# Delta net stage: inverse in two groups, scan without W and U, output norm token-major

## The reference, cut to what matters

```python
a_strict = jnp.einsum('bhnid,bhnjd->bhnij', kb, k) * decay * (idx[:, None] > idx[None, :])
rhs = jnp.concatenate([v * beta[..., None], kb * jnp.exp(gc)[..., None]], axis=-1)
sol = lax.linalg.triangular_solve(a_strict + jnp.eye(C, dtype=F32), rhs, left_side=True, lower=True, unit_diagonal=True)
u, w = sol[..., :dv], sol[..., dv:]
attn = jnp.einsum('bhnid,bhnjd->bhnij', q, k) * decay
def step(S, inp):
    v_new = u_i - jnp.einsum('bhcd,bhde->bhce', w_i, S)
    o = (jnp.einsum('bhcd,bhde->bhce', q_i * jnp.exp(g_i)[..., None], S)
         + jnp.einsum('bhij,bhje->bhie', a_i, v_new))
    S = (S * jnp.exp(g_last)[..., None, None]
         + jnp.einsum('bhcd,bhce->bhde', k_i * jnp.exp(g_last[..., None] - g_i)[..., None], v_new))
    return S, o
```

## Time and profile before

| | |
|---|---|
| median of 3 runs | 2707.88 us (2705.71 to 2708.81) |
| span of the profiled execution | 2700.6 us |
| TensorE busy | 2612.6 us, 97% of the span |
| VectorE, ScalarE, GpSimd busy | 1011.4, 660.8, 501.4 us |

### The profile page before, as it was taken

One profiled execution on the slowest core, in us unless ns is written; L12 is line 12 of the kernel. 1 busy time (PEld: TensorE's weight loads), 2 busy tenths in 40 slices (PEclk: granted clock), 3 DMA queues, 4 the chain that ended last, 5 costly groups with the idle time before them and its releaser, 6 DMA issues. The chain is left out here.

```text
span 2700.6 us, 43745 instructions
## 1 busy us (share of the span) xinstructions
PE 2612.6 (97%) x17527; PEld 1664.5 (62%) x17528; DVE 1011.4 (37%) x2331; ACT 660.8 (24%) x1383; POOL 501.4 (19%) x465
## 2 busy tenths in 40 slices
PE   6999999979999999999999999999997999999998
PEld 3565565555555555556677677767744458568485
DVE  2354455346676763013444344434432110010100
ACT  3354454121222210115222332323202111110110
POOL 0111111132332315222223122312200100000000
PEclk7999999989999999999999999999998999999999
DMA  8234224113333342201011101110209997695841
GB/s 250 69 78 128 68 68 126 48 52 119 109 109 115 105 118 64 65 22 34 3 32 33 32 2 33 33 32 2 72 17 348 344 343 226 186 296 176 253 130 28
DMA packets 321292, 295.01 MB, mean 109 GB/s; under 512 B 5920, under 2 KB 285600, under 8 KB 321024
## 3 DMA queue, kind: packets, MB, share of 16 engines
q1 hardware_dynamic: 315648, 273.17, 33.3%
q0 software_dynamic: 4352, 15.60, 2.4%
q10 hardware_dynamic: 1152, 4.19, 0.4%
HBM read 279.83 MB, written 11.53 MB: 108 GB/s over the span
## 5 line engine op out<-in xcount | busy, mean ns | idle before, releaser
L2363 PE MATMUL bank<-hidden,weight_ring 128*128 128x512 f32 (+1 forms) x768 | 308.7, 536 | 1.8 <-ACT work L2707 1.8
L1293 PE MATMUL bank<-hidden,weight_ring 128*128 128x384 f32 x704 | 237.7, 491 | 4.9 <-ACT hidden L415 4.9
L648 PE MATMUL bank<-weight_ring,hidden 128*128 128x384 f32 x672 | 237.2, 496 | 1.6 <-ACT work L795 1.4
L1439 DVE SCALAR_TENSOR_TENSOR weight_ring<-weight_ring,silu_c 128x256 f32<-128x256 f32 x308 | 213.7, 735 | 5.5
L1293 PEld LDWEIGHTS bank<-hidden,weight_ring 128*128 128x128 f32 x704 | 132.9, 191 | 93.5 <-issue 6.7
L2363 PEld LDWEIGHTS bank<-hidden,weight_ring 128*128 128x128 f32 x768 | 134.9, 190 | 82.4 <-issue 68.1
L1293 PE MATMUL bank<-weight_ring 128*128 128x384 f32 x528 | 181.6, 494 | 0.3 <-DVE work L1447 0.3
L648 PEld LDWEIGHTS bank<-weight_ring,hidden 128*128 128x128 f32 x672 | 121.7, 191 | 92.1 <-issue 15.7
L1810 PE MATMUL bank<-work,weight_ring 128*128 128x224 f32 x768 | 147.7, 354 | 0.0
L1810 PEld LDWEIGHTS bank<-work,weight_ring 128*128 128x128 f32 x768 | 144.1, 190 | 1.9 <-ACT work L1892 1.6
L1293 PEld LDWEIGHTS bank<-weight_ring 128*128 128x128 f32 x528 | 99.3, 192 | 70.1 <-issue 5.9
(11 more groups left out here) (386 smaller groups left out, 3994.8 us busy)
## 6 DMA issues: line engine op xcount, KB each, us to landing
weight_ring<-in_moe_w_in SPq DMA_DIRECT2D x64, 1024.0 KB, 9.5
weight_ring<-in_ada_w SPq DMA_DIRECT2D x38, 1024.0 KB, 5.3
weight_ring<-in_ffn_w_in SPq DMA_DIRECT2D x44, 512.0 KB, 4.9
hidden<-in_moe_w_out SPq DMA_DIRECT2D x8, 2816.0 KB, 10.0
residual<-in_moe_w_out SPq DMA_DIRECT2D x8, 2816.0 KB, 14.6
work<-in_moe_w_in SPq DMA_DIRECT2D x16, 1024.0 KB, 8.4
weight_ring<-in_na_w_qkv SPq DMA_DIRECT2D x24, 512.0 KB, 9.5
weight_ring<-in_gdn_w_qkv SPq DMA_DIRECT2D x24, 512.0 KB, 5.4
```

The costliest lines, as they stand in the source:

```text
L648: mm = nc.tensor.matmul(m.psum[6][:, 0:3 * P], m.H[:, k, t * P:(t + 1) * P], weights(u)[:, k, :], start=(k == 0), stop=(k == KD - 1))
L1293: mm = nc.tensor.matmul(bank[:, 0:HT], w[:, k, :], t[:, k, :], start=(first and k == 0), stop=(last and k == HK - 1), skip_group_check=True)
L1439: nc.vector.scalar_tensor_tensor(out=out, in0=ada_slab[:, k, :], scalar=by, in1=out, op0=ALU.mult, op1=ALU.add).then_inc(acc_ok, 1)
L2363: mm = nc.tensor.matmul(B[b][:, c0:c0 + t1 - t0], W[:, s, k, :], m.H[:, k, t0:t1], start=(k == 0), stop=(k == KD - 1))
```

## The change

1. **Inverse.** LEVELS = 6 becomes GROUPS = 2. The first mask gives U = I - A0 as before. A group then does Y = AM T, and three nested products (`xa`, `xb`, `xc`: X = U - Y U, X = U - Y X, U = U - Y X) and the same last product for T; after two groups one more Y and one `u`. GpSimd makes four masks per direction, not six, each in its own buffer.
2. **Scan without W and U.** `wt`, `cu`, `kb`, `vb` and the two turns `at0`, `at1` go. A step is now `ks` (keys times state), `x` on VectorE (V - e^g k S), `tx` on TensorE (inverse times x), `vn` on ScalarE (scaled copy), `kv`, `st`.
3. **k and q of a chunk as one stationary operand.** From step 4 on `ks` multiplies keys and queries (`KQ`, 128 columns) with the state at once; the query half is taken by `oa` on ScalarE (steps 4 to 7) or `od` on VectorE (steps 8 to 11), and `eg`, `QE` and their exponentials go.
4. **Output norm token-major.** Squares with sums on ScalarE, the scaling on GpSimd, four transposes (`turn_out`), and the gate's product on VectorE; `norm_sums` and `norm_rows` go.
5. The streams are rewritten in a new order; the output weights of the last turn are loaded in two batches.

```diff
-LEVELS = 6
+GROUPS = 2
...
+                def ks(s):
                     if not scan:
                         return
-
+                    for d in range(2):
+                        t, half, _, c, _ = place(s, d)
+                        pe.wait_ge(dve_scan_step, VS.before(h, f"st{s - 1}.{d}"))
+                        if s < 4:
+                            k0 = t * P + CH * half
+                            mm = nc.tensor.matmul(B[SCAN + d][c, 0:P], keys(h - 1)[:, k0:k0 + CH], state[:, d, :], start=True, stop=True)
+                        else:
+                            mm = nc.tensor.matmul(B[SCAN + d][:, 0:P], keys_and_queries(h - 1, t, half), state[:, d, :], start=True, stop=True)
+                        mm.then_inc(pe_scan_step, TS.step(f"ks{s}.{d}"))
...
+                def tx(s):
...
+                            pe.wait_ge(dve_scan_step, VS.before(h, f"x{s}.{d}"))
+                        x = xs[c, d, :] if s else V[(h - 1) % 2][c, t, :]
+                        nc.tensor.matmul(B[SCAN + d][c, 2 * P:3 * P], UF[c, n, :], x, start=True, stop=True)\
+                            .then_inc(pe_scan_step, TS.step(f"tx{s}.{d}"))
...
+                        _, _, n, c, _ = place(s, d)
+                        pe.wait_ge(act_scan_step, SS.before(h, f"vn{s}.{d}"))
+                        if s >= MEET:
+                            pe.wait_ge(dve_scan_step, VS.before(h, f"od{s}.{d}"))
+                        if s < STEPS - 1:
+                            nc.tensor.matmul(B[SCAN + d][:, P:2 * P], kd[c, n, :], vn_[c, d, :], start=True, stop=True)\
...
+                            t, _, _, c, other = place(s, d)
+                            nc.tensor.matmul(B[OUT][other, t * P:(t + 1) * P], AT[c, 4 * d + t, :], vn_[c, d, :], start=(s == 4), stop=True,
...
+                def turn_out():
...
+                    pe.wait_ge(pool_scan_step, GS.before(h, "on"))
                     for t in range(4):
...
+                        mm = nc.tensor.transpose(B[GATE][:, t * P:(t + 1) * P], otok[:, t, :], ident)
...
+                    mm = nc.tensor.transpose(B[(0, 2)[t // 4]][:, (t % 4) * P:(t % 4 + 1) * P], keys(h)[:, t * P:(t + 1) * P], ident)
                 mm.then_inc(pe_step, TE.step("kt"))
-                pe.wait_ge(dve_step, VE.after(h, "right_vc"))
+                ks(5)
...
                 mm.then_inc(pe_step, TE.step("kk"))
-                ws(5)
-                project(1, 0, 0, CTX, TOK, 4, 6)
-                kv(5)
-                project(1, 0, 0, CTX, TOK, 6, 8).then_inc(pe_step, TE.step("q"))
-                ws(6)
+                tx(5)
                 pe.wait_ge(act_step, SC.after(h, "Kc"))
                 project(2, 0, 2, CTX, TOK, 0, 2)
+                kv(5)
+                project(2, 0, 2, CTX, TOK, 2, 4)
+                ks(6)
+                project(2, 0, 2, CTX, TOK, 4, 6)
+                tx(6)
+                project(2, 0, 2, CTX, TOK, 6, 8).then_inc(pe_step, TE.step("v"))
                 kv(6)
...
+                gate_part(0, 2)
+                ks(7)
+                pe.wait_ge(act_step, SC.after(h, "silu_q1"))
+                pe.wait_ge(dve_step, VE.after(h, "a1"))
...
+                ks(8)
+                pe.wait_ge(dve_step, VE.after(h, "U0"))
+                turn(0, U, 0, "tt0")
...
+                def first(g, d):
...
+                    multiply(2 * d, AM[g + 1], T, d, f"y{g}.{d}")
+
+                def second(g, d):
+                    pe.wait_ge(act_step, SC.after(h, f"Y{g}.{d}"))
+                    multiply(2 * d + 1, Y, U, d, f"xa{g}.{d}")
+
+                def third(g, d):
+                    pe.wait_ge(dve_step, VE.after(h, f"Xa{g}.{d}"))
+                    multiply(2 * d, Y, X, d, f"xb{g}.{d}")
+
+                def fourth(g, d):
+                    pe.wait_ge(dve_step, VE.after(h, f"Xb{g}.{d}"))
+                    multiply(2 * d + 1, Y, X, d, f"xc{g}.{d}")
+                    multiply(2 * d, X, Y, d, f"t{g}.{d}")
...
+                third(0, 0)
+                ks(11)
+                third(0, 1)
+                tx(11)
+                fourth(0, 0)
+                kv(11)
+                fourth(0, 1)
...
-                            b = (1, 0)[d] + 2 * half
-                            mm = nc.tensor.matmul(blocks(b, TILES)[:, n, :], kb[c, TILES * d + n, :], U[c, TILES * d + n, :],
-                                                  start=True, stop=True)
-                    mm.then_inc(pe_step, TE.step(f"wt{d}"))
...
-                        for c in HALF_ROWS:
-                            mm = nc.tensor.matmul(B[b][c, at_:at_ + P], U[c, TILES * d + n, :], vb[c, TILES * d + n, :], start=True, stop=True)
-                    mm.then_inc(pe_step, TE.step(f"cu{d}"))
+                    third(1, d)
...
+                    pe.wait_ge(act_step, SC.after(h, f"Y{GROUPS}.{d}"))
+                    pe.wait_ge(dve_step, VE.after(h, f"Xc{GROUPS - 1}.{d}"))
+                    multiply(1 + d, Y, U, d, f"u.{d}")
+                turn_out()
...
+                def oa(s):
...
+                        act.wait_ge(pe_scan_step, TS.before(h, f"ks{s}.{d}"))
+                        nc.scalar.activation(oacc[other, t, :], B[SCAN + d][other, 0:P], ACT.Identity, scale=coef[other, EGS, h - 1, n:n + 1])\
+                            .then_inc(act_scan_step, SS.step(f"oa{s}.{d}"))
+
+                def vn(s):
...
+                    for d in range(2):
+                        _, _, n, c, _ = place(s, d)
+                        act.wait_ge(pe_scan_step, TS.before(h, f"tx{s}.{d}"))
+                        nc.scalar.activation(vn_[c, d, :], B[SCAN + d][c, 2 * P:3 * P], ACT.Identity, scale=hr[(h - 1) % 2][c, 0, n:n + 1])\
+                            .then_inc(act_scan_step, SS.step(f"vn{s}.{d}"))
...
+                oa(5)
                 act.wait_ge(pe_step, TE.after(h, "kt"))
                 act.wait_ge(pool_step, GP.before(h, "kd1"))
                 for t in range(4):
-                    op = nc.scalar.activation(k_sq[:, t, :], B[0][:, t * P:(t + 1) * P], ACT.Square, accum_out=ss_k[:, t:t + 1])
+                    op = nc.scalar.activation(k_sq[:, t, :], B[0][:, t * P:(t + 1) * P], ACT.Square, accum_out=nk[h % 2][:, t:t + 1])
                 op.then_inc(act_step, SC.step("sq_k"))
+                vn(5)
+                for t in range(2):
+                    op = nc.scalar.activation(k_sq[:, 4 + t, :], B[2][:, t * P:(t + 1) * P], ACT.Square, accum_out=nk[h % 2][:, 4 + t:5 + t])
+                op.then_inc(act_step, SC.step("sq_kc"))
+                act.wait_ge(act_step, SC.after(h, "sq_kc"))
+                nc.scalar.activation(nk[h % 2], nk[h % 2], ACT.Sqrt, bias=const(m, C_EPS, 1)).then_inc(act_step, SC.step("root_k"))
                 nc.scalar.copy(K[:, 0:4, :], B[0][:, :].rearrange("p (n t) -> p n t", n=4)).then_inc(act_step, SC.step("K"))
-                for t in range(2):
-                    op = nc.scalar.activation(k_sq[:, 4 + t, :], B[2][:, t * P:(t + 1) * P], ACT.Square, accum_out=ss_k[:, 4 + t:5 + t])
-                op.then_inc(act_step, SC.step("sq_kc"))
                 nc.scalar.copy(K[:, 4:6, :], B[2][:, 0:2 * P].rearrange("p (n t) -> p n t", n=2)).then_inc(act_step, SC.step("Kc"))
-                act.wait_ge(act_step, SC.after(h, "sq_kc"))
-                nc.scalar.activation(ss_k, ss_k, ACT.Sqrt, bias=const(m, C_EPS, 1)).then_inc(act_step, SC.step("root_k"))
...
-                    nc.vector.tensor_tensor(T[:, of(d), :], blocks(3, TILES), DM[:, of(d), :], ALU.mult).then_inc(dve_step, VE.step(f"ad{d}"))
-                vn(7)
-                for d in range(2):
-                    dve.wait_ge(pe_step, TE.after(h, f"at{d}"))
-                    nc.vector.tensor_tensor(A[:, of(d), :], blocks(d, TILES), spread(hr[:, 0, of(d)], TILES, CH), ALU.mult)\
-                        .then_inc(dve_step, VE.step(f"a{d}"))
...
+                nc.vector.tensor_scalar(qn[h % 2], B[3][:, CTX:CTX + 4], float(GD * GD * EPS), None, ALU.mult).then_inc(dve_step, VE.step("qn"))
+                x(8)
+                od(8)
                 for d in range(2):
                     dve.wait_ge(pool_step, GP.after(h, f"am0.{d}"))
-                    nc.vector.tensor_tensor(T[:, of(d), :], same(ident64, TILES), AM[:, of(d), :], ALU.subtract)\
...
+                    nc.vector.tensor_tensor(U[:, of(d), :], same(ident64, TILES), AM[0][:, of(d), :], ALU.subtract).then_inc(dve_step, VE.step(f"U{d}"))
...
+                x(11)
+                od(11)
+                take_b(0, 0)
+                take_b(0, 1)
                 sum_o()
-                level(2)
-                value_rows(0)
-                value_rows(1)
-                level(3)
-                value_rows(2)
+                take_c(0, 0)
+                take_c(0, 1)
...
+                for d in range(2):
+                    take_a(1, d)
+                for d in range(2):
+                    take_b(1, d)
```

(16 more changed lines are left out.)

829 lines of the change are left out of this document (414 added, 415 removed).

## The result

The changed kernel takes 2715.75 us (median of 7 runs, 2714.88 to 2720.19), the kernel before, beside it on the same chip, 2707.88 (2705.71 to 2710.42): ratio 1.0033, 95% interval 1.0023 to 1.0043. The forecast was 2686 and faster. The value lies inside the range, by 1.25 us, and the sign was wrong. In the profiled executions the spans are 2714.0 and 2700.6 us, a difference of 13.4. Of the four executions of the later run e9_all one, 3257.59 us at a granted clock of 0.745, was in a slower state of the chip and counts in no ratio.

What follows compares the result with a forecast made beforehand. TensorE's issue time bounds a middle turn: 91.5 us less 13.1 of work and the 0.17 wait, plus 9.7 of waits and 1.4 of clock, makes 89.3. With turn 0 (-4) and the last (-1): 2686 us, range 2640 to 2717.

Steps and rivals of the forecast that it cites:

- What bounds it, and that the cover decides: A middle turn is TensorE's issue time; removing its instructions pays only while waits between the engines keep their cover.
- Kc: TensorE's wait for ScalarE's copy of the transposed keys, ahead of the v projection: 3.3 us a turn.
- a1: TensorE's wait behind `ks` of step 7 for VectorE's second a tile: 1.7 us a turn.
- U0: TensorE's wait behind `ks` of step 8 for VectorE's first U tile: 1.7 us a turn.
- `x` of step 5: TensorE's wait for VectorE's x, which stands behind q's convolution: 0.4 us a turn.
- so I add 1.4 a turn: TensorE's clock halves behind the Kc wait, slowing the work that follows: 1.4 us a turn.
- the clock falls at every wait: Rival, chance 0.12: the clock also falls at a1, U0 and in the inverse; 93.5 us a turn, 2721, slower.
- dm1's wait: `tx` replaces `kv` and the table load loses the cover of `eg`: 0.4 us a middle turn.
- 0.06 per change: Price of a change of TensorE's tiling mode between projections and scan steps: 0.06 us, judged a small thing.
- Turn 0: The first turn loses work, its own waits and slow stretch but gains new waits and clock loss: net -4 us.
- work kept: Rival, chance 0.10: the waits overlap more than laid out; 2598 with none, 2640 with half of them.
- longer chain of the scan: Rival, chance 0.06: the scan's four hops for two set the pace; the gain is gone, 2708.

Runs made afterwards that it cites:

- e9_all: e6_both and e8_o_late together, plus two VectorE subtractions of the inverse moved ahead of od(11) and sum_o; 2611.78 us, ratio 0.9649 to the kernel before.
- e3_fill: Changed kernel with four unread 512-column matmuls in TensorE's queue ahead of the wait for the copy of the keys; 2701.1 us, ratio 0.9974 to the kernel before.
- e6_both: Changed kernel with keys transposed ahead of half of q's projection and a and U tiles earlier on VectorE; 2630.33 us, ratio 0.9725 to the kernel before.
- e10_kv_twice: e9_all with the pair of state products kv of steps 0 to 10 issued twice; 2627.55 us, ratio 0.9705 to the kernel before.
- e8_o_late: Changed kernel with the output products o of a step right ahead of the next step's tx; 2696.69 us, ratio 0.9967 to the kernel before.
- e1_kc_order: Changed kernel with ScalarE copying the transposed keys out before it takes the root of their norms; 2695.91 us, ratio 0.9952 to the kernel before.
- e2_kt_early: Changed kernel with keys transposed ahead of half of q's projection, ScalarE's squares and copies and VectorE's x(5) earlier; 2661.55 us, ratio 0.9828 to the kernel before.

## Why the prediction was wrong, step by step

- **What bounds it, and that the cover decides:** right. All time went and came in TensorE's turns.
- **The waits:** right in place and releaser, and nearly in size: Kc, a1, U0 and `x` of step 5 forecast 3.3 + 1.7 + 1.7 + 0.4 = 7.1, measured 7.6. The half microsecond is Kc's: ScalarE's chain ended 6.1 us behind `kt` for 5.4 laid out, and TensorE came to wait at 2.3 for 2.0.
- **The clock, "so I add 1.4 a turn":** this is the term that failed most, 3.4 measured. I took turn 0's loss of 1.3 us, where 3.62 us of work (1272.23 to 1275.85) take 2.30 otherwise, as the price of any fall. Behind the Kc wait of turn 2 the slow stretch is longer: 7.19 us (1429.72 to 1436.91), which take 4.52 in e3_fill (1427.38 to 1431.90). That fall is 2.7. And I let only one wait count; behind the 1.62 wait of a1 the clock fell in every second turn, 1.4 each time. The rival "the clock falls at every wait" was half right: in the middle turns no fall followed U0's 1.71 or the waits inside the inverse, and in place of its four falls of 1.4 there were one of 2.7 and half a one of 1.4. It had the sign and nearly the turn (93.5 for 93.8), with 0.12 of the chance, but by another sum. The Trainium skill, page TensorE: Matmul & The Clock Gate, section HAM oscillation, says a pause is paid again in slowed work behind it; e3_fill confirms this here, with 2.7 us behind a pause of 3.8.
- **`kv` and `o` taken as unchanged:** mis-sized. From start to start `kv` and `o` took 0.32 + 0.27 in the kernel before, where both used a 64-row, full-width part of the array, and 0.42 + 0.37 in the changed one, where `o` uses a quarter. Summed over a turn from start to start, `kv` and `o` went from 6.3 to 7.5 us (e6_both): 1.2. `ks` came to 5.5 for 5.1 laid out, the inverse with its waits to 19.8 for 19.4, and dm1's wait to 0.7 for 0.4: another 1.1. The query products were 4.1 and not 3.9, and `tx` was priced well, 0.37 between projections and 4.2 in all for 4.4; with the turned matrices these take back some 0.5. With roundings that is 82.7 for a forecast of 78.2 + 0.4 + 2.2 = 80.8 without the other waits: 1.9. Of the 0.20 a step for `kv` and `o` perhaps only half is the change of shape: `o` also streams 128 columns where it streamed 64 (64x64 in the earlier trace rows, 64x128 above). By the 0.22 of a pair of 128 columns the other 64 would be 0.11, an estimate that no run tests; `kv`, with the same operands' shapes, rose by 0.10.
- **"0.06 per change":** too small. The page TensorEngine Tiling of the Trainium skill, section Key Properties, says that a change of mode drains the array and that tiles work in parallel. Rows here fit both: 0.20 us around a pair and 0.1 in the projection on either side (e10_kv_twice, e6_both), and an `o` pair for nothing beside `tx` (e8_o_late). My 0.06 a change was a misreading: it set 1.92 from start to start against half of a row's own 3.72, though that run of 16 rows takes 3.65 from start to start (1575.35 to 1579.00 in the kernel before) and has a change at either end. I weighed the rule's first half and judged it small, since the row of `ws` held such changes already; the change between `kv` and `o`, which no row of before had, I did not look for.
- **Sum for a middle turn:** work and small waits +1.9, the four waits +0.5, clock +2.0: 4.4 of the 4.5 us.
- **Turn 0:** -2.3 for -4. The clock fell behind the Kc wait of 3.3 and behind U0's of 2.2, as laid out, but for more than the 2.7 of both: the v projection takes 10.1 us (1258.72 to 1268.78) where it takes 7.1 in e6_both (1254.86 to 1261.92), and the clock is at 0.50 again from 1272.6 to 1281.0. In e6_both this turn is 58.6 us instead of 69.6.
- **From the span to the time:** I added 7.3 us, the distance of the median from the span of one profiled execution, which was a quick one: in later executions of the kernel before the time is 2.1 above the span. For the changed kernel the same execution has a time of 2715.75 and a span of 2714.0, 1.75 apart. The sum was therefore off by 34, not 30, and that the value lies inside the range is luck: with 2 us in place of 7.3 the range would have ended at 2712.
- **The rivals:** work kept, no; longer chain of the scan, no (e6_both has turns of 82.7 with that chain in it).

Open: why the clock falls behind a 1.62 us wait in one turn and not in the next. The falls at the Kc wait and at the a1 wait, of seven turns each, were 7 and 4 in the changed kernel, 6 and 7 in e1_kc_order, none and 6 in e3_fill, none and 3 in e2_kt_early, and no rule comes out of that.
